# v projection as seven-product quads, u weight blocks loaded ahead of the last chunks, y and k scratch in rows of 1 KB

## What is computed

```python
h = x @ W_in          # -> q | k | v | g | a_low | u | z | gate_a | gate_b
# branch A: gated linear attention, 4 heads, dk 128, dv 256
log_a = log_sigmoid(a_low @ w_gate_up + b_gate) / 16
o   = gla_chunked(q * 128**-0.5, k, v, log_a)      # S_t = diag(a_t) S_{t-1} + k_t^T v_t ; o_t = q_t S_t
y_a = rms_norm_heads(o, gn_w) * silu(g)
# branch B: causal trailing means over 2/4/8/16 tokens minus the token, per group a 256x256 map
p   = pool(u) @ pool_w + pool_b
y_b = p * pool_scale * silu(z)
merged = sigmoid(gate_a) * (y_a @ W_a) + sigmoid(gate_b) * (y_b @ W_b)
out = layer_norm(2**0.25 * x + merged @ W_o)
```

## Time and profile before

| | before |
|---|---|
| three runs, us | 599.94, 601.82, 596.96; median 599.94 |
| the profiled execution, us | 600.11 |
| its span on the slowest core (core 7), us | 598.3 |
| busy share of the span: PE / PEld / DVE / ACT / POOL | 97% / 47% / 72% / 47% / 9% |
| bytes moved by DMA, MB | 60.18, in 64901 packets, 53392 of them under 512 B |

### The profile page before, as it was taken

One profiled execution on the slowest core, in us unless ns is written; L12 is line 12 of the kernel. 1 busy time (PEld: TensorE's weight loads), 2 busy tenths in 40 slices (PEclk: granted clock), 3 DMA queues, 4 the chain that ended last, 5 costly groups with the idle time before them and its releaser, 6 DMA issues.

```text
span 598.3 us, 10048 instructions; the slowest of 8 cores (591.9 to 598.3 us)
## 1 busy us (share of the span) xinstructions
PE 578.2 (97%) x2978; PEld 279.0 (47%) x2978; DVE 430.9 (72%) x835; ACT 279.0 (47%) x590; POOL 56.0 (9%) x121
## 2 busy tenths in 40 slices
PE   7999999999999999899999999999999999999994
PEld 2434455555555554344444444444444434455553
DVE  2488848776766687689777887565875519988797
ACT  2489966556565654244333323566633203223223
POOL 1110002221212130000001000100000000100010
PEclk9999999999999999899999999999999999999998
DMA  8999973585533439800034301696300053454452
GB/s 234 316 172 171 171 134 71 99 129 92 77 58 55 79 51 149 119 2 0 5 33 39 68 1 30 114 165 114 72 1 1 1 170 124 164 166 147 140 184 106
DMA packets 64901, 60.18 MB, mean 101 GB/s; under 512 B 53392, under 2 KB 53520, under 8 KB 62544
## 3 DMA queue, kind: packets, MB, share of 16 engines
q0 software_dynamic: 7184, 21.50, 22.5%
q1 hardware_dynamic: 40480, 33.57, 22.2%
q10 hardware_dynamic: 17184, 4.47, 4.0%
HBM read 61.10 MB, written 14.16 MB: 126 GB/s over the span
## 4 chain that ended last, share of the span: by engine, by line
PE 87%; DMA 7%; DVE 3%; issue 1%; SPq 1%; ACT 0%; POOL 0%; DVEq 0%; ACTq 0%; POOLq 0%
PE pb L858 24%; PE pb L623 19%; PE pb L952 14%; PE pb L1375 8%; PE pb L409 5%; PE pb L429 4%; PE pb L1327 3%; PE pb L1335 3%; DMA yscr<-A 3%; DMA A<-head 1%; PE pb L1359 1%; PE pb L663 1%; PE pb L668 1%; PE pb L680 1%; PE pb L985 1%
## 5 line engine op out<-in xcount | busy, mean ns | idle before, releaser
L623 PE MATMUL pb<-A,xT 128*128 128x512 bf16 x384 | 90.2, 379 | 0.0
L952 PE MATMUL pb<-A,ws 128*128 128x512 bf16 x256 | 64.1, 379 | 0.0
L1390 ACT ACTIVATE junk<-xT 128x512 bf16<-128x512 f32 (+1 forms) x33 | 20.2, 612 | 80.3 <-DVE xT L1384 80.2
L623 PEld LDWEIGHTS pb<-A,xT 128*128 128x128 bf16 x384 | 36.2, 98 | 35.4 <-issue 0.2
L701 ACT ACTIVATE A<-A,eblast 128x256 bf16<-128x256 f32 x60 | 30.5, 508 | 47.5 <-DVE A L696 42.3
L863 ACT COPY sgm_t<-pb 128x512 f32<-128x512 f32 x54 | 31.6, 585 | 31.2 <-PE pb L858 29.8
L858 PE MATMUL pb<-A,ws 128*128 128x512 bf16 x184 | 45.6, 379 | 0.0
L858 PE MATMUL pb<-A 128*128 128x512 bf16 x168 | 42.8, 385 | 0.4 <-DVE A L777 0.2
L858 PE MATMUL pb<-xT,A 128*128 128x512 bf16 x144 | 37.0, 386 | 3.3 <-DVE A L889 2.7
L952 PEld LDWEIGHTS pb<-A,ws 128*128 128x128 bf16 x256 | 25.0, 98 | 30.2
L929 ACT ACTIVATE sgm_t<-sgm_t 128x512 f32<-128x512 f32 x24 | 15.1, 630 | 47.5 <-DVE sgm_t L889 24.7
(11 more groups left out here) (159 smaller groups left out, 1011.6 us busy)
## 6 DMA issues: line engine op xcount, KB each, us to landing
ws<-wts POOLq DMA_DIRECT2D x11, 1024.0 KB, 13.0
A<-head SPq DMA_DIRECT2D x32, 256.0 KB, 8.9
A<-x SPq DMA_DIRECT2D x16, 512.0 KB, 5.1
out<-xT SPq DMA_DIRECT2D x15, 512.0 KB, 3.2
A<-wts POOLq DMA_DIRECT2D x6, 1024.0 KB, 28.5
yscr<-A ACTq DMA_DIRECT2D x32, 128.0 KB, 2.6
kscr<-A SPq DMA_DIRECT2D x12, 128.0 KB, 3.0
xT<-xt POOLq DMA_DIRECT2D x2, 512.0 KB, 11.6
```

What stands on the lines that cost most here:

```text
L623: PE(lambda e, k=k, c=c, bank=bank, W=W: e.matmul(pb[bank][:, :], xTc(c, k), W[:, k, :], start=(k == 0), stop=(k == KC - 1)), r=[B], w=[bb ...
L952: PE(lambda e, k=k: e.matmul(pb[bank][:, :], W.ap[:, k, m * 128:(m + 1) * 128], aT[:, k, tb * 512:(tb + 1) * 512], start=(k == 0), stop=(k ...
```

## The change

The v projection of two chunks (256 tokens) by 1024 columns becomes one quad: 28 matmuls of 128x512 in place of 32. Its weight sums (`gv_sums`, DVE) are made once, in the gate stage and at the start of the loop; its input sums (`gu_sum`, five of 128x512 a pair, DVE) once a pair. g stays plain. The loop works by pairs of chunks, with the units of the next pair put by a table into the four steps of a pair; the first pair's v and g stand ahead of the loop. v leaves PSUM by two ACT copies and two DVE subtractions a pair, where DVE copied four tiles. ACT adds three copies a pair. The second of the two state scalings of a step goes to POOL. The k transposes of the first four chunks are made in two blocks (`kd_block`). k^T v is left out in the last chunk, whose state nobody reads.

Each row of the y and k scratch is now 1 KB (512 bf16 values) where it was 256 B; the transposing reads take 128 columns of such rows. y has four buffers in place of three. The writes Y(29), Y(30) and Y(31) move from ACT's queue to SP's.

u0 is loaded as before; u1 goes into A4 in step 17, and not into ws1 ahead of the loop. `wp_part` of the first block moves to steps 25 to 27, the 32 plain u matmuls (`direct_u`) to steps 28 to 31, and `wp_part` of the second block between the products of the first u quad. The sums for the first u quad are spread over steps 26 to 31 (`tail_ops`). The load of wa0 follows wp1, those of ga0 and ga1 come later, and the slots' roles are exchanged.

The core of the diff:

```diff
-    kscr = nc.dram_tensor("kscr", [NT, 512, 128], BF16).ap()
-    yscr = nc.dram_tensor("yscr", [4, KC, 512, 128], BF16).ap()
+    kscr = nc.dram_tensor("kscr", [4, 512, 512], BF16).ap()
+    yscr = nc.dram_tensor("yscr", [4, 2, 512, 512], BF16).ap()
...
+        def vg_evac(kind, c, blk, src, sB, neg=False):
+            o, oB = vg_seg(kind, c, blk), b_vg[kind][c % 4][blk]
+            ACT(lambda e: e.activation(o, src, AF.Silu if kind else AF.Copy), r=sB, w=[oB],
+                extra=vg_free(kind, c, blk))
...
+        def gu_sum(i, pair):
+            c = 2 * pair
+            x1, x2 = [xT[:, c // 4, :, (c % 4 + j) * 128:(c % 4 + j + 1) * 128] for j in range(2)]
...
+            UENG(lambda e: e.tensor_tensor(GU[i], a, b, op), w=[b_GU[i]])
+
+        def gq(kind, pair, i):
...
+            for k in range(4):
+                PE(lambda e, k=k: e.matmul(pb[bank][:, :], u(k), x(k), start=(i in (5, 2) and k == 0), stop=k == 3,
+                                           skip_group_check=True), r=ub + xb, w=[bb[bank]])
+            if i == 5:
+                ACT(lambda e: e.copy(pb[bA][:, :], pb[bB][:, :]), r=[bb[bB]], w=[bb[bA]])
+            elif i in (2, 0):
+                t = 2 if i == 2 else 1
+                ACT(lambda e: e.copy(GT[t], pb[bank][:, :]), r=[bb[bank]], w=[b_GT[t]])
+            elif i in (3, 1):
...
+                DVE(lambda e: e.tensor_tensor(o, a, b, ALU.subtract), r=[bb[bank], b_GT[t]], w=[oB],
+                    extra=vg_free(kind, c, blk))
...
+            else:
+                vg_evac(kind, c + 1, i == 4, pb[bank][:, :], [bb[bank]])
+
+        OB = [n % 2 for n in range(28)] + [2, 3, 6, 5]
...
+            for j in range(2 if c < NT - 1 else 0):
...
-                ACT(lambda e, j=j, h=h: e.activation(
-                    Sbf_s[hp][(c + 1) % 2][:, j, :], S_f[hp][:, j, :], AF.Copy, scale=eblast[:, c, h:h + 1]),
+                o, i, sc = Sbf_s[hp][(c + 1) % 2][:, j, :], S_f[hp][:, j, :], eblast[:, c, h:h + 1]
+                (POOL if j else ACT)(
+                    (lambda e, o=o, i=i, sc=sc: e.tensor_scalar(o, i, sc, None, ALU.mult)) if j else
+                    (lambda e, o=o, i=i, sc=sc: e.activation(o, i, AF.Copy, scale=sc)),
...
-            P.add("act", lambda e: e.dma_start(
-                out=yscr[tb, hp * 4:hp * 4 + 4, (c % 4) * 128:(c % 4 + 1) * 128, :].rearrange("q t f -> t q f"),
-                in_=yb_s[n % 3].rearrange("p j (i f) -> p (j i) f", i=2)),
-                reads=[b_ybs[n % 3]], writes=[b_ysc[tb][c % 4][hp]], lane=f"ys{n % 3}")
+            P.add("sp" if n > 28 else "act", lambda e: e.dma_start(
+                out=yscr[tb, hp, (c % 4) * 128:(c % 4 + 1) * 128, :], in_=yb_s[n % 4].rearrange("p j f -> p (j f)")),
+                reads=[b_ybs[n % 4]], writes=[b_ysc[tb][c % 4][hp]], lane=f"ys{n % 4}")
...
+            for j, units in enumerate(((5, 2), ("a0", "a1"), (0, 6), (3, "b0"), ("b1", 1), ("c0", "c1"), (4, "d0"), ("d1",))):
+                for u in units:
+                    put(n + j // 2, j % 2, *(g[u] if isinstance(u, str) else (gq, 0, pair, u)))
...
+            if n == 17:
+                ld(wu[1], "u1", extra=lastops(b_kT[0:8]))
...
-        S_wp1 = Sums(wp[1], e_aps(A4, 8192), wp1_ops + free_g)
-        S_ga0 = Sums(R[0], e_aps(A4, 11264), free_g)
+        S_wp1 = Sums(wp[1], e_aps(A4, 8192), free_g)
+        S_ga0 = Sums(R[2], e_aps(A4, 11264), free_g)
...
+        def wp1_done():
+            as_slot(wp[1], b_wp[1])
+            ld(R[1], "wa0", extra=[P.last["pe"]])
+            i = sum(x in xs0 for x in bg)
+            bg[i:i] = S_wp1.ops()
+
+        fill.extend(lambda k=k: wp_part(1, k, k + 1) for k in range(KC))
+        fill.append(("hook", wp1_done))
...
-        qu0[2].post += [lambda: ld(R[2], "ga1", extra=lastops(wp[0].all)), pools((1, 3))]
+        qu0[2].post += [lambda: ld(R[2], "ga0", extra=lastops(wp[0].all)), pools((1, 3))]
```

More of the change, by code:

```diff
@@ L607, in build_program @@
         b_sTs = [Buf() for _ in range(2)]
-        b_ybs = [Buf() for _ in range(3)]
+        b_ybs = [Buf() for _ in range(4)]
         b_Sbf = [[Buf() for _ in range(2)] for _ in range(2)]
@@ L654, in st_T1S, with kd_block @@
                 r=[bb[5], b_lt], w=[b_sTs[s]])
+        def kd_block(i):
+            bank = 5 + i
+            for j in range(8):
+                c, h = 2 * i + j // 4, j % 4
+                PE(lambda e, j=j, c=c, h=h: e.transpose(
+                    pbT[bank][:, j * 128:(j + 1) * 128], kbT[:, h, c * 128:(c + 1) * 128], ident[:]),
+                   r=[b_kbb[h][0], b_ident], w=[bb[bank]])
+            DVE(lambda e: e.tensor_copy(kd[i], pbT[bank][:, 0:1024]), r=[bb[bank]], w=[b_kds[i]])
         def st_UO1(n):
@@ L752, in build_program @@
         fill = []
-        def lastops(bufs):
-            out = []
-            for b in bufs:
-                by = {}
-                for o in b.r:
-                    by[o.lane] = o
-                out += list(by.values()) + ([b.w] if b.w is not None else [])
-            return out
         class Once:
@@ new lines, in direct_u @@
+        def direct_u(p, half):
+            dc, tb = ((2, 0), (2, 1), (0, 0), (0, 1))[p]
+            bank = DBANK[p]
+            for k in range(half * 4, half * 4 + 4):
+                PE(lambda e, k=k: e.matmul(
+                    pb[bank][:, :], wp[0].ap[:, k, dc * 128:(dc + 1) * 128], xTb(tb, k),
+                    start=(k == 0), stop=(k == KC - 1)), r=[b_wp[0][k]] + wp[0].all, w=[bb[bank]])
+            if half:
+                u_evac(dc, tb, bank)
+        DBANK = (0, 7, 4, 7)
+        put(25, 1, lambda: wp_free.append(P.last["pe"]))
@@ L1120, in build_program, with on_dve @@
-        w0[4][1]()
-        xs1[2][1]()
-        wp1_ops = as_slot(wp[1], b_wp[1])
+        ld(R[0], "u0", extra=readers(b_wq))
+        xs1 = wino_x(1)
+        def on_dve(ops):
+            for op in ops:
+                (op[1] if isinstance(op, tuple) else op)()
+        tail_ops = {26: [xs1[0]], 27: [xs1[1]]}
+        for i in (2, 0, 6, 3, 4):
+            b_GU[i].r = [P.last["dve"]]
+            if i in (6, 3):
+                for op in vsum[2:4] if i == 6 else vsum[4:]:
+                    op()
+            gu_sum(i, 0)
```

327 lines of the change are left out of this document (199 added, 128 removed).

## The result

The changed kernel takes 593.01 us (median of 4 runs, 592.8 to 593.06), the kernel before beside it 599.7; the ratio is 0.989, with an interval from 0.985 to 0.9931. The forecast was 592.5 with a range from 587.5 to 598.5. So the time came out as forecast; of its two large terms one was exact and one was too small by 3 us, and a gain that was not foreseen lay against it, so the closeness is in part luck.

A forecast was written before the change was run, and what follows sets the result against it. PE's instruction count was taken as the bound, plus PE's waits on the slowest core. From 600.1 us, -6.9 - 0.4 - 0.8 - 4.5 + 0.5 + 0.5 + 4.0 = -7.6 gave 592.5 us, range 587.5 to 598.5.

The forecast's parts named there:

- two large terms: Matmuls removed from the loop's pairs, -6.9 us; stop and slow clock at the new junction behind the loop, +4.0 us.
- PE's work: Chunk loop: each pair loses 4 of 32 v matmuls, 16.9 to 16.04 us, -6.9 in all; last chunk's k^T v, -0.4.
- Rival D: Loop pairs stay at 16.9 us, set by a chain through PE, ACT's copy and DVE's subtraction; 599.4 us, chance 0.13.
- The waits of `wp_part`: PE's waits for the banks of `wp_part` (L985) go, as its parts are spread out: -0.8 us.
- The waits added: First v quad ahead of the loop and first u quad each wait for an ACT copy: +0.5 us each.
- POOL's scalings: Four state scalings a loop pair on POOL, 0.7 us each, at most 8.3 of 16.04 us busy; cost 0.
- rival C: Loop pairs: POOL's scalings hold DVE up until DVE is the bound; 614 us at 1.5 us each, chance 0.08.
- The junction: First u quads to wp1 quads: Y(31), caught by wa0's load, stops PE 2.5 us, slow clock 1.5 more: +4.0 us.
- E: Time at which PE leaves the chunk loop, 216.56 us on core 7 before; the junction's events are counted from it.
- rival B: Junction: Y(31) waits for all transposes and the whole load, landing at E + 24.3; costs 7.7, 596.2 us, chance 0.14.
- rival A: Junction: Y(31) gets through before the load moves, E + 15, no stop; 588.5 us, chance 0.25.
- The old junction: First u quads to wp1 quads before: waits of 0.61 and 2.17 and 1.7 of slow clock go, -4.5 us.

## Why the prediction was right, and where it was not

**PE's work: right.** The matmuls removed are 7.3 us of PE's time, and the pairs took it: 16.0 forecast and measured, and 16.9 with the product put back. Rival D is out.

**The waits of `wp_part`: right.** L1078 has no idle time; a wait of 0.24 us at the plain u matmuls (L1173, for DVE) stands in the same steps.

**The waits added: too dear.** Of the 0.5 in the first u quad 0.25 was found (core 6), of the 0.5 ahead of the loop some 0.3, in two gaps of 0.13 and 0.14 (before the rows at 85.47 and 87.33 us).

**POOL's scalings: priced too low, and still hidden.** I took 0.7 us from the nearest row; one takes 0.93 in the loop. They lengthen the sums that read two SBUF operands, by 80 and 200 ns on the mean. This is the contention of rival C. That it exists, as the Trainium skill, SBUF — State Buffer, section "Who interferes with whom", states, the rows of the sums with and without POOL's work bear out. That the one shuts the other out for its whole length they do not (POOL and DVE timelines, core 6):

```profile
119.95 0.93 POOL L804 TENSOR_SCALAR A<-A,eblast 128x256 bf16<-128x256 f32 x1 [1.17 <-ACT A L805]
```

```profile
120.08 0.62 DVE L690 TENSOR_TENSOR mask_t<-xT 128x512 bf16<-128x512 bf16 x1
120.62 0.41 DVE L460 TENSOR_TENSOR A<-A 128x512 bf16<-128x512 bf16 x1
```

The sum begins behind the scaling and ends ahead of it, 0.2 us late, and the product after it is not late at all. The prediction also counted the state updates and the y products among the instructions with two SBUF inputs; their rows show one operand from PSUM, and they take 475 and 481 ns beside POOL's scalings where the earlier trace rows has 476 and 482. So it came nowhere near C's price: DVE is busy for 13.2 us of 16.0 in the fuller of the two pairs above.

**The junction: the mechanism right, the size wrong.** The stop, its place, its cause and both issue times were as worked out (Y(31) at E + 12.1 for 12.4, wa0 at E + 11.5 for 11). The step that failed is the landing, for which I took E + 20.8 from a range of 20 to 23. My own numbers gave no reason for a low value: a load issued at E + 11 that takes 11.0 us lands at E + 22, and what it has caught lands behind it. (The load of 11.0 in the earlier trace rows did not run alone, as I had it: SP's queue moved 1409 packets of y's transposes beside it between 242 and 253 us. The shortest loads of these runs take 8 us.) The write landed at E + 23.1. So the stop was 4.07 us for 2.5. The clock took more as well: between the rows at 232.9 and 245.02 us, 24 matmuls (5.2 us at full pace) took 12.1, so core 6 lost 7.0 us there where my sum had 4.0; rival B had 7.7. The rule of the Trainium skill on queues (DMA: Bandwidth & Descriptors, section "Queues, rings and completion order") would have let the small write through in groups, and rival A with it; no core shows that, since on all eight the write landed 0.2 us behind the load.

**What lay against it.** The old junction was worth 4.8 us on core 7 (241.21 to 250.32 us, 20 matmuls) where I had 4.5. And waits of later quads, which I had not costed, are shorter or gone. Core 7 before, and core 6 after (PE timelines):

```profile
260.50 1.02 PE L858 MATMUL pb<-xT,A 128*128 128x512 bf16 x4 [0.53 <-DVE A L889]
...
374.85 1.02 PE L858 MATMUL pb<-xT,ws 128*128 128x512 bf16 x4 [1.07 <-DVE ws L777]
...
402.64 1.02 PE L858 MATMUL pb<-xT,junk 128*128 128x512 bf16 x4 [0.87 <-DVE sgm_t L889]
```

```profile
395.05 1.02 PE L950 MATMUL pb<-xT,junk 128*128 128x512 bf16 x4 [0.51 <-DVE sgm_t L981]
...
486.30 1.46 PE L1480 MATMUL pb<-xT,ws 128*128 128x512 bf16 x6 [1.82 <-DVE xT L1537]
```

The waits of all eight cores agree with these to 0.3 us, and with 0.17 us for each restart they are some 2 us less. DVE released PE in all three, so the order of DVE's work, which came out otherwise with the new slots, is the likely cause; that was not tried. The wait for x is on core 6 as it was on core 7, 0.5 us longer.

**The sum.** E fell from 216.56 to 212.58, by 4.0, for a forecast of 4.2 (6.9 + 0.4 + 0.8 - 0.5, with 6.9 of u's matmuls moved ahead of E and 3.5 of wp1's behind it). From E to the end the slowest core takes 3.0 less, for a forecast of 3.4 (6.9 - 3.5 + 4.5 - 4.0 - 0.5). The second figure is right by luck: two errors of 2 to 3 us with opposite signs. On the mean of the eight cores E fell by 4.7 and the rest by only 0.7, since the stop that half of the cores had before now stands on all.

## What to carry to other kernels

A small write that takes 2 us alone can take a whole load's time beside one: list for each transfer that something waits for what else is moving when it is issued, and what stands ahead of it on its queue, and move the write, not the load. Where a stop of PE is removed or made, count what the clock does behind it too: here 2.8 us beside a stop of 4. A faster stage shows the next late thing on the slowest of eight cores, so half of a gain can go there; look at what the other cores wait for before putting a number to it.

## What the runs showed of the hardware

- A y write of 128 packets issued beside a load landed 0.2 us behind the load on all eight cores, 10.0 to 11.5 us after its issue, where it took 1.7 with no load beside it and no transposes ahead; with 512 packets it landed 0.4 us behind the load on core 3.
- Transposing reads and loads can hold each other up for 20 us and more: 1426 transposing packets took 105% of the engines' time in 22 us, and the loads beside them 17.5 and 32.9 us, on core 0 of an execution on whose core 3 the same loads took 8.2 and 10.2. The cause is open.
- PE's clock fell to 0.82 on the mean of the 19.5 us behind a stop of 4 us, with matmuls at half pace from 237.4 to about 244 us, and stayed at 1.00 when extra matmuls filled the stop.
- DVE's sums of two SBUF operands took 498 and 621 ns beside POOL's scalings, and 418 and 416 without them; the y products, which read PSUM, did not change (481 ns with them, 482 in the earlier trace rows).
